# Reordered mixers and joins of a two-block trunk, with two output tiles in memory of their own

## The reference, cut to what matters

```python
h = modulate(x, norm_g[i, 0], ada[:, 0, 0], ada[:, 0, 1])
x = x + 0.5 * ada[:, 0, 2, None, :] * swiglu(h, ffn_w13[i, 0], ffn_w2[i, 0])
h = modulate(x, norm_g[i, 1], ada[:, 1, 0], ada[:, 1, 1])
if i % N_MIXERS == 0:
    y = mlstm_mixer(h, a_w_in[j], a_conv_w[j], a_conv_b[j], a_b_if[j], a_norm_g[j], a_w_out[j])
else:
    y = diff_attn_mixer(h, cos, sin, b_w_in[j], b_lam[j], b_norm_g[j], b_w_out[j], lam_init)
x = x + ada[:, 1, 2, None, :] * y
h = modulate(x, norm_g[i, 2], ada[:, 2, 0], ada[:, 2, 1])
x = x + 0.5 * ada[:, 2, 2, None, :] * swiglu(h, ffn_w13[i, 1], ffn_w2[i, 1])
```

```python
hh = hh * lax.rsqrt(jnp.mean(hh * hh, -1, keepdims=True) + EPS)
hh = hh.reshape(nb, S, A_V) * norm_g.astype(jnp.float32)
y = (jax.nn.sigmoid(o.astype(jnp.float32)) * hh).astype(h.dtype)
return y @ w_out
```

## Time and profile before

| what | value |
|---|---|
| median of 3 runs | 2005.21 us (2004.33 to 2005.86) |
| the profiled execution, its time | 2003.45 us |
| its span, first to last instruction | 2001.7 us |
| TensorE busy | 1947.8 us, 97% of the span |
| VectorE busy | 1080.7 us, 54% |
| ScalarE busy | 654.3 us, 33% |
| granted TensorE clock, mean | 0.993 |
| mixer A, from its v halves to its output projection's first group | about 457 to 628 us of the span |
| mixer B, from its first v half to the same point | about 1408 to 1602 us |

### The profile page before, as it was taken

How to read it: one execution, slowest core, us unless ns; L and a number is a source line. 1 busy time by engine, 2 the same in 40 slices (tenths; PEclk the granted TensorE clock), 3 DMA queues, 4 the chain that set the end, 5 groups by cost and what they waited for, 6 DMA issues and landing times.

```text
span 2001.7 us, 26124 instructions
## 1 busy us (share of the span) xinstructions
PE 1947.8 (97%) x9466; PEld 1628.9 (81%) x9466; DVE 1080.7 (54%) x1611; ACT 654.3 (33%) x953; POOL 2.7 (0%) x14
## 2 busy tenths in 40 slices
PE   5999999999999999999999999999999999999998
PEld 5888888887678888888898888889776698888887
DVE  6765553385367655553365555537686674333333
ACT  3332232243433432232242222223344443232321
POOL 0000000000000000000000000000000000000000
PEclk9999999999899999999999999999999999999999
DMA  7665643233111456553336556332211123322332
GB/s 283 227 217 190 199 138 100 86 97 104 50 56 64 151 189 196 190 162 100 102 99 208 190 189 193 104 99 87 95 64 53 43 93 111 101 94 92 87 94 84
DMA packets 76597, 254.29 MB, mean 127 GB/s; under 512 B 8280, under 2 KB 10456, under 8 KB 76408
## 3 DMA queue, kind: packets, MB, share of 16 engines
q1 hardware_dynamic: 76048, 250.71, 39.2%
q10 hardware_dynamic: 488, 2.75, 0.3%
HBM read 251.33 MB, written 2.10 MB: 127 GB/s over the span
## 4 chain that ended last, share of the span: by engine, by line
PE 90%; DVE 5%; DMA 2%; ACT 1%; issue 1%; SPq 1%; DVEq 0%; ACTq 0%
PE acc L494 20%; PE acc L496 20%; PE acc L495 20%; PE outp L494 8%; PE outp L496 8%; PE outp L495 8%; DVE w_lo L1261 1%; DMA early_ada<-ada 1%; PE outp L714 1%; PE stat L494 1%; PE stat L496 1%; PE stat L495 1%; ACT w_hi L894 1%; PE acc L800 1%; DVE buf L1326 1%
## 5 line engine op out<-in xcount | busy, mean ns | idle before, releaser
L494 PE MATMUL acc<-h_hi,w_hi 128*128 128x512 f32 (+1 forms) x1952 | 718.4, 368 | 7.9 <-DVE h_lo L1273 4.6
L495 PE MATMUL acc<-h_lo,w_hi 128*128 128x512 f32 (+1 forms) x1952 | 710.0, 364 | 0.0
L496 PE MATMUL acc<-h_hi,w_lo 128*128 128x512 f32 (+1 forms) x1952 | 709.8, 364 | 0.0
L1261 DVE TENSOR_TENSOR w_lo<-raw,w_hi 128x1024 fp32r<-128x1024 f32 (+2 forms) x369 | 413.7, 1122 | 449.8 <-ACT w_hi L894 438.5
L894 ACT ACTIVATE w_hi<-raw 128x1024 fp32r<-128x1024 f32 (+2 forms) x369 | 358.9, 973 | 391.3 <-PE outp L496 286.2
L494 PEld LDWEIGHTS acc<-h_hi,w_hi 128*128 128x128 f32 x1952 | 369.3, 189 | 72.7 <-DVE h_lo L1273 6.8
L495 PEld LDWEIGHTS acc<-h_lo,w_hi 128*128 128x128 f32 x1952 | 369.4, 189 | 58.6 <-issue 1.0
L496 PEld LDWEIGHTS acc<-h_hi,w_lo 128*128 128x128 f32 x1952 | 369.4, 189 | 58.0
L494 PE MATMUL outp<-g_hi,w_hi 128*128 128x512 f32 (+1 forms) x792 | 290.5, 367 | 0.0
L495 PE MATMUL outp<-g_lo,w_hi 128*128 128x512 f32 (+1 forms) x792 | 289.4, 365 | 0.0
L496 PE MATMUL outp<-g_hi,w_lo 128*128 128x512 f32 (+1 forms) x792 | 289.4, 365 | 0.0
(11 more groups left out here) (207 smaller groups left out, 1171.9 us busy)
## 6 DMA issues: line engine op xcount, KB each, us to landing
raw<-w SPq DMA_DIRECT2D x176, 512.0 KB, 3.4
ada_raw<-ada SPq DMA_DIRECT2D x128, 512.0 KB, 4.3
raw<-w SPq DMA_DIRECT2D x64, 384.0 KB, 3.2
raw<-w SPq DMA_DIRECT2D x64, 320.0 KB, 2.9
raw<-wa SPq DMA_DIRECT2D x33, 512.0 KB, 3.4
raw<-wb SPq DMA_DIRECT2D x32, 512.0 KB, 3.4
early_ada<-ada SPq DMA_DIRECT2D x8, 1024.0 KB, 18.7
x<-xT ACTq DMA_DIRECT2D x1, 2048.0 KB, 13.3
```

What stands on the lines that cost most here:

```text
L494: pe.matmul(bank, a_hi, b_hi, start=start, stop=False)
L495: pe.matmul(bank, a_hi, b_lo, start=False, stop=False)
L496: return pe.matmul(bank, a_lo, b_hi, start=False, stop=stop)
L1261: dve.tensor_tensor(w_lo[s][:, 0:n], raw[base % RAWS][:, 0:n], w_hi[s][:, 0:n].bitcast(F32), ALU.subtract).then_inc(lo_ready, 1)
```

## The change

No product is added or left out. The change moves instructions in the lists of PE, ACT and DVE, and adds one semaphore and four buffers:

- Joins: `norm_sum(n, 1)` goes behind the first 4 tiles of s = 2, `spread_rstd(n, 1)` behind the first 2 tiles of s = 3.
- The v halves: a new semaphore `v_tile_done` counts token tiles 0 to 2 as they are finished, and the copies out wait for it, ahead of ACT's last high part.
- Mixer A: `o_tile(1)` goes ahead of `scores(0)`, and the others follow; `mix(3)` goes ahead of `o_tile(7)` with the first two factors inside it; tiles 0 and 1 of the output get memory of their own (`y_hi`, `y_lo`, over buffers that are free by then), so that their products need not wait for h; the sums and factors of heads 2 and 3 go between products; DVE's and ACT's lists are ordered to that.
- Mixer B: `keep_qk` goes ahead of `high_part` in the first group; in the loop `head_sum` goes behind `scores`, `inverse` ahead of `rope`, one low part ahead of `rope` at n = 11, and `pair` to the end of a step; the products of tiles 0 and 1 go around `turn(15)`, `head_sum(2)` ahead of `mix(3)`.

The diff, cut to its core:

```diff
@@ first_group (PE)
-                    if half == 0 and n:
-                        norm_sum(n, 1)
...
                         for k in range(KT):
                             product(s, k, half)
-                        if half == 0 and s == 2:
-                            spread_rstd(n, 1)
...
+                            if half == 0 and n and s == 2 and k == 3:
+                                norm_sum(n, 1)
+                            if half == 0 and s == 3 and k == 1:
+                                spread_rstd(n, 1)
@@ v_half (PE) and v_evac (ACT, DVE)
+                        if m == 3 and tt < ST - 1:
+                            last.then_inc(v_tile_done, 1)
...
-                for m in range(4):
+                for m in range(3):
                     high_part(U + m + 4)
-                act.wait_ge(unit_done, U + 4)
                 for tt in range(2):
+                    act.wait_ge(v_tile_done, before + tt + 1)
                     act.activation(dst[:, tt, half * 512:half * 512 + 512], acc[:, tt, :], ACT.Copy)\
                        .then_inc(acc_free[tt], 1)
+                high_part(U + 7)
@@ mixer_a (PE)
                 spread_row(6, 20)
+                o_tile(1)
                 pe.wait_ge(a_qk_ready, 8)
                 scores(0)
-                o_tile(1)
+                o_tile(2)
                 scores(1)
                 mix(0)
-                o_tile(2)
                 scores(2)
...
+                mix(3, {1: lambda: early_factor(0), 2: lambda: early_factor(1)})
+                o_tile(7)
+                pe.wait_ge(den_read, 4)
+                head_sum(2, aux)
                 pe.wait_ge(a_std_ready, 2)
...
+                early = [(y_hi[k][:, :], y_lo[k][:, :]) for k in range(2)]
+                for k in range(2):
+                    for s in range(3):
+                        if k == 0 and s < 2:
+                            pe.wait_ge(a_factor_ready, s + 1)
+                        out_product(U + 25, T_A_OUT, Q_A_OUT, s, k, early)
+                for k in range(2):
+                    out_product(U + 25, T_A_OUT, Q_A_OUT, 3, k, early)
@@ mixer_b (PE)
                 for n in range(4 * HEADS):
                     scores(n)
+                    if n in (8, 12):
+                        head_sum(n // 4 - 2)
...
-                    if n in (7, 11):
-                        head_sum(n // 4 - 1)
...
                 mix(2)
+                for s in range(2):
+                    for k in range(2):
+                        out_product(U + 24, T_B_OUT, Q_B_OUT, s, k)
                 turn(15)
+                for s in range(2, 4):
+                    for k in range(2):
+                        out_product(U + 24, T_B_OUT, Q_B_OUT, s, k)
+                head_sum(2)
                 mix(3)
@@ mixer_b (ACT)
                 for t in range(4):
-                    high_part(U + t + 4)
                     act.wait_ge(unit_done, U + t + 1)
                     keep_qk(t, t)
+                    high_part(U + t + 4)
@@ mixer_b (DVE)
+                    if n == 15:
+                        make(0)
+                        low_part(U + 24)
+                        make(1)
+                        low(0)
+                        low_part(U + 25)
                     maxima(n)
+                    if n in (8, 12):
+                        inverse(n // 4 - 2)
+                    if n == 11:
+                        low_part(U + 12 + n)
+                    if n < 12:
+                        rope(4 + n)
+                    if n < 11:
+                        low_part(U + 12 + n)
                     if n in (7, 11):
                         pair(n // 4 - 1)
```

249 lines of the change are left out of this document (144 added, 105 removed).

## The result

| | changed kernel | before, same set |
|---|---|---|
| median | 1987.11 us (1986.67 to 1989.55, 4 runs) | 2005.28 us |
| again, later | 1986.60 us (1984.45 to 1987.25, 4 runs) | 2006.01 us (2003.09 to 2010.26) |
| the profiled execution, its span | 1989.55 us, 1987.7 us | 2003.45 us, 2001.7 us |

The ratio is 0.9912 with a 95% interval of 0.9895 to 0.993: 18.2 us faster, where 18 were forecast. The total fell on the forecast, but one of its terms, the clock in mixer A, did not do what the forecast said. So the sum is gone through term by term, and then the clock is taken apart by experiments.

What follows compares the result with a forecast made beforehand. PE was taken as the bound nearly everywhere, so only its waits and clock loss could be won: gains of 22 us less 4 us for the joins, 18 us net, giving 1987 us, range 1980 to 1995.

Steps and rivals of the forecast that it cites:

- the clock in mixer A: Behind mixer A's row spreads: of 5.1 us lost to the lower clock, 1.7 us would be won back.
- v halves: Second v half of mixer A and the same stretch in mixer B: waits go, gains of 2.0 and 4.35 us.
- Mixer A behind them: Mixer A after its v halves: gain 3.0 us up to the heads and 3.7 us in its tail.
- three parts: Clock cost in mixer A's slices from 500 to 530 us: 1.5, 1.9 and 1.7 us, one part of 1.7 taken back.
- The fall at 610: Lower clock in mixer A's tail, 610 to 620 us, costing 1.7 us; the clock there would be 1.00.
- v half and loop of B: Mixer B: gain 4.35 us in the v half and 2.8 us in the loop, with a new `head_sum(0)` wait.
- Tail of B: Mixer B's tail: products fill waits and the clock's fall goes; 3.13 + 3.4 - 0.45 = 6.1 us gained.
- Joins: The six joins: a later spread makes them longer, costing 4.0 us together, bounds 0 and 8.
- DVE's chain from the spread on sets the end: In a join, PE and DVE arrive together, so a later spread makes the join longer by as much.
- Rival A: The clock stays up through mixer A's row spreads: 3.4 us more gain, 1983.5 us; chance 17%.
- Rival B: Lower clock stays in mixer A, mixer B's loop wins nothing, tails get new waits: 1990 to 1994 us; chance 23%.
- Rival D: Slower: the clock falls at a mixer's end and an output projection runs at 1.2 GHz, 22 us more each; chance 3%.

Runs made afterwards that it cites:

- late copies: The changed kernel with ACT and DVE copying v only after the whole half, as before the change: 1995.19 us.
- wide row spreads: The changed kernel with row spreads over 128 partitions instead of 4: 1982.80 us; with the copies of v as before too, 1988.81 us.
- late products: The changed kernel with mixer B's 24 product matmuls of tiles 0 and 1 behind `turn(15)`, `head_sum(2)` and `mix(3)`, as before: 1994.89 us.

## Why the prediction was right, and where it was not

- **v halves.** Right: 2.36 and 4.52 us for 2.0 and 4.35. All idle time there went, which the late copies confirm (2.1 and 1.7 us come back with them).
- **Mixer A behind them.** The waits went as forecast: without the clock the stretch from 502.81 fell from 133.9 to 130.2 us, 3.7 us (1.35 + 1.6 + 0.4 had been counted). The clock was the step that failed in the profile. The forecast counted three parts, one for each slice of 10 us, where there are two falls (3.4 and 1.7 us), and took one part at the row spreads, 1.7 us, to go with the gap. In the profile the loss rose to 6.8 us, in later ones it was 5.1 (three times) and 3.4 (twice); before it was 5.1, and with the late copies 6.8. The argument that a cost would stay, since the small matmuls stay and PE was busy ahead of the second fall, was right; that one part would go with the gap is not shown: the mean is 4.8 us in six profiles without the gap and 6.0 in two with it, and the wide row spreads behind the same gap lost nothing. What brings the clock down there is the 4 partitions. The fall at 610 went, in every profile, as forecast.
- **v half and loop of B.** The mechanisms and the new waits were right, to 0.15 us. In the profiled execution the loop gave 1.2 and not 2.8 us because the clock fell once, behind the new wait of `head_sum(0)`; with that taken off it gave 2.9. The forecast priced that wait at 1 us and did not ask what it might do to the clock. That the wait brings the fall is not shown (three profiles of eleven).
- **Tail of B.** Right: 6.32 for 6.1 us. That the clock's fall there belonged to the waits and what stands around them, the least sure part of the term, is what the late products show.
- **Joins.** Right: 4.1 for 4.0 us, by undoing it 3.8, with n = 0 uncertain by some 0.4 us. "DVE's chain from the spread on sets the end" holds only because PE and DVE were level there; in the other direction PE is the bound after half a microsecond.
- **Rival A** (the clock stays up) is refuted, and with it the 3.4 us. **Rival B** was true in one part, the clock's cost, and wrong in the others. **Rival D**'s long fall never came.
- **Why the median hit 1987** although the profiles say 14 us: the profiled execution of before was among the fast ones of its kernel (2003.45 against 2005.28) and that of the changed kernel the slowest of its four. The later pair of medians gives 19.4 us. The sum from one profile could not be better than the clock's scatter, about 2 us on either side; that the median agreed to 0.1 us is luck, that each term but the clock agreed to 0.4 us is not.

## What to carry to other kernels

Where PE is the bound, idle time in front of it can be added up term by term to a few tenths of a microsecond, if each new wait and each later start is priced too; an edit that fills a wait but delays what another engine's chain starts from (the joins here) can cost more than it fills. Look at the granted clock behind every group of narrow or tiny matmuls, not only behind gaps, and try making them wide: over 128 partitions with zeros the row spreads here cost the same time and kept the clock. Compare profiles with the clock's loss taken off, and try undoing the parts one by one, since one of six here was a loss.

## What the runs showed that was not expected

- Eight float32 matmuls on 4 partitions, in two rows of four, bring the clock to 1.2 GHz with PE busy before, during and after: 3.4 to 6.8 us lost in every profile that has them in rows. The same number on 128 partitions, of real data, ones or zeros, loses nothing in five profiles.
- A gap of 1.35 us did not lower the clock by itself (one profile, the late copies with wide row spreads), nor did one of 3.18 us between products (the kernel before).
- A lone float32 matmul between products of the split kind costs 1.05 us and 0.1 us more on either neighbour, against two passes of about 0.43 us in a row of four.
- Starting the spread of a join early was worth 0.5 us where a wait could be filled and cost 0.3 us in n = 2 and 5, where the sum had filled a wait for the weight and no longer did.
- In every profile the clock also falls in the last 15 us of the kernel, where PE waits for DVE. It costs little: the last two spreads stand 7.27 to 7.29 us apart in every one, and from the last spread to the end of the span it is 7.35 or 7.36 us in the nine profiles where the fall begins behind that spread, and 7.87 or 7.88 us in the five where it begins ahead of it. So a mean clock over the span overstates what is to be won.
